# A hybrid GLA, SSD and mixture-of-experts block on one core: attention state per 128 tokens, and expert operands 128 columns wide

## The chip, the core and the metric

The kernel runs on one core of a Trainium2 chip. The metric is device microseconds (us) of one launch; the kernel before takes 2227.91 us (median of three runs, 2227.89 to 2229.29). A core has a matrix engine (TensorE; PE in the profile, its weight loads PEld), three engines for elementwise work (VectorE or DVE, ScalarE or ACT, GpSimd or POOL), a queue engine that issues most transfers (SyncE or SP), and 16 DMA engines between HBM and the on-chip memory. The engines run at the same time, each through its own instructions in program order, and wait for one another by semaphores only.

## What is computed

The reference, cut to what the change touches:

```python
def gla_scan(q, k, v, log_a):                 # one direction, per head; 64 tokens per chunk
    def step(state, inp):
        b = jnp.cumsum(gc, axis=1)            # cumulated log gates inside the chunk
        b_mid = b[:, c // 2][:, None]
        s = where(mask, (qc * exp(b - b_mid)) @ (kc * exp(b_mid - b)).T, 0)
        o = s @ vc + (qc * exp(b)) @ state
        kd = kc * exp(b[:, -1:] - b)
        state = state * exp(b[:, -1]) + kd.T @ vc
...
def moe(xn, w_router, b_router, w1, b1, w2, b2):   # top 4 of 32 experts per token
    def expert_block(xblk, e):
        hdn = xblk @ w1[e] + b1[e]            # 1024 -> 2048
        gate = minimum(hdn[..., :1024], 7.0)
        lin = clip(hdn[..., 1024:], -7.0, 7.0)
        return gate * sigmoid(1.702 * gate) * (lin + 1.0) @ w2[e] + b2[e]   # 1024 -> 1024
```

There are 512 tokens, 4 GLA heads (key width 128, value width 256, both directions), an SSD mixer, and 32 experts. A state that is kept once per 128 tokens gives the same output as one per 64, if the products between the two halves of the 128 are formed as well.

## The kernel before

All data are float32. Large products are made from splits: a matrix is copied to a rounded high half (ACT) and the rest is kept as a low half (DVE subtracts), and three matmuls of 512 columns (high by high, high by low, low by high) stand for one. Products inside the attention are plain float32, and each of them is two matmul records in the trace.

**The mixer stage.** The input projection is cut into 112 *units* of 1024 x 128 weights. Each is loaded by SP (three slots), split by ACT (`split_high`) and DVE (`split_low`), and used by PE in a *piece* of 24 matmuls of 512 columns. SP loads unit n once the low half of unit n - 3 is made. ACT takes each piece out of PSUM (`piece_take`), and a piece waits until the piece two before it was taken. Groups of four units (quads) are needed together.

**The GLA heads** run between pieces, in an order written out by hand (`HEAD_PIECES` for PE and ACT, `HEAD_SPLITS` for DVE). In a head, DVE forms differences of the cumulated gates, ACT takes eight exponentials of 128 x 512, DVE multiplies them with q or k. PE makes scores (L451), transposes the decayed keys (L442), multiplies the masked scores with v (L465), and then walks through eight chunks of 64 tokens, forward and backward together: a state matmul (L479), DVE's update of the state (L582, L585), and the state's share of the output in the next step (L476). The two buffers of exponentials are single, so a head's exponentials wait for the last output matmul of the head before.

**The expert stage** is a loop over 32 experts (a *pass*). The tokens of an expert are gathered by POOL (at most 96 per round, `CAP`), transposed by PE and split into `rows_high` and `rows_low`; these are the stationary operands, with 96 columns each for 8 chunks. The weights stream in as tiles of 128 x 2048 (1 MB) through a ring of eight slots: 8 tiles for the product up, 4 for the product down of the expert before. ACT makes `w_high`, DVE `w_low`, each with three slots, so ACT splits a tile once PE is done with the tile three before. PE runs 12 matmuls of 512 columns per tile. SP loads a tile when DVE has split the tile eight before. Between the tiles DVE clamps gate and linear part (L2020, L2021), makes `rows_low` of the next expert (L1991), the product of gate and linear part (L2032) and `act_low` (L2051). The order on DVE around them is

```python
            gate_dve(v, it)          # both clamps
            rows_dve(v, it + 1)
            if not is_first(it):
                for j in range(UP + 2, TILES):   # the third and the fourth tile of the product down
                    low_dve(v, it, odd, j)
            glu_dve(v, it)
```

After the loop, the last expert's product down is made from four more tiles. Its splits on DVE stand behind `places_dve`, which waits until the previous expert's rows were scattered, and on ACT behind `down_act`, the row scaling of the previous expert.

Of the kernel before, what the change touches and what calls it, by code (L numbers as in the profile page):

```python
# [14 lines left out]
P = 128  # L15
# [30 lines left out]
CAP = 96  # L46
ROUNDS = -(-SEQ // CAP)
# [49 lines left out]
def build(nc, x, norm_mix_g, w_in, fw2_f, fb_f, fw2_b, fb_b, gla_norm_g, conv_w, conv_b, dt_bias_f,  # L97
          dt_bias_b, a_log_f, a_log_b, ssd_d, ssd_norm_g, w_up_gla, w_up_ssd, w_out, norm_ffn_g,
          w_router, b_router, w1, b1, w2, b2, norm_final_g, out):
    with ExitStack() as ctx:  # L100
# [160 lines left out]
        def piece_take(act, n):  # L261
# [4 lines left out]
            if kind in ("q", "k"):  # L266
                if i == 1 and kind == "q":
                    act.wait_ge(scan_ok, 4 + 2 * HEADS)
                if i >= 2:
                    act.wait_ge(g_qk, 8 * (i - 1))  # L270
# [80 lines left out]
        def dts(i):  # L351
# [23 lines left out]
        g_e = [[take(SEQ) for _ in range(4)] for _ in range(2)]  # L375
        at_gd = used[0]
        g_d = [[take(SEQ) for _ in range(2)] for _ in range(2)]
        kd_n = take(2 * SEQ).rearrange("p (d t n) -> p d t n", d=2, t=NT)
        s_m = take(SEQ)
        s_w = take(SEQ // 2)  # L380
        o_junk = take(DV)
        g_st = [take(DV) for _ in range(2)]
        dec = take(2 * NCH).rearrange("p (d c) -> p d c", d=2)
# [18 lines left out]
        LAST, MID = (CH - 1, 0), (CH // 2, CH // 2 - 1)  # L402
# [3 lines left out]
        HEAD_PIECES = ({"start": (8, 9), "score": (), "kd": (), 1: (), 4: (10,), "end": (11,)},  # L406
                       {"start": (12, 13), "score": (14,), "kd": (15,), 1: (16,), 4: (17,), "end": (18, 19)},
                       {"start": (20, 21), "score": (), "kd": (), 1: (), 4: (22,), "end": (23,)},
                       {"start": (24, 25), "score": (26,), "kd": (27,), 1: (28,), 4: (29,), "end": (30, 31, 32, 33)})
# [4 lines left out]
        def o_at(c):  # L414

            t, half = divmod(c, KG)
            return slice(half * CH, (half + 1) * CH), 4 + t // 2, slice((t % 2) * DV, (t % 2 + 1) * DV)
# [12 lines left out]
        def gla_pe(pe, h):  # L430
# [4 lines left out]
            def transposes(d):  # L435
                pe.wait_ge(g_qk, h * 8 + 4 * d + 4)
# [4 lines left out]
                for t in range(NT):  # L441
                    last = nc.tensor.transpose(ps[:, 3, t * P:(t + 1) * P], g_e[d][3][:, t * P:(t + 1) * P], ident[:])  # L442
                last.then_inc(kd_ps, 1)
            transposes(0)
            pe.wait_ge(g_qk, h * 8 + 8)
            for d in range(2):
                for c in range(NCH):
                    rows = o_at(c)[0]
                    to = d * 4 * CH + (c // KG) * CH
                    i = slice(c * CH, (c + 1) * CH)  # L450
                    last = nc.tensor.matmul(ps[rows, 2, to:to + CH], g_e[d][1][:, i], g_e[d][0][:, i], start=True, stop=True)  # L451
# [6 lines left out]
            pe.wait_ge(s_sel, h * 2 + 2)  # L458
# [1830 lines left out]
```

## Time and profile before

| | before |
|---|---|
| runs, median (range) | 2227.91 us (2227.89 to 2229.29) |
| profiled execution: its time, its span | 2231.43 us, 2229.7 us |
| PE, PEld busy | 2046.1 us (92%), 1490.9 us (67%) |
| DVE, ACT, POOL busy | 1603.5 us (72%), 1219.5 us (55%), 263.1 us (12%) |
| moved by DMA | 541.09 MB, mean 243 GB/s |

The span is one execution from first to last instruction; the execution's own time is 1.7 us longer. The heads of the GLA lie at about 84 to 352 us of the span, the expert stage at about 985 to 2200 us. A timeline row gives start, length, engine, line and operation, `out<-in` by the program's names (`temps` is the scratch area in which nearly all of the mixer stage lives, `ps` is PSUM), the shapes, and in brackets the idle time before it with what ended it. A record of a matmul is longer than the distance to the next one, since matmuls overlap: the pace of PE is read from starts.

### The profile page before, as it was taken

The page shows a single profiled execution, that of the slowest core. Times are in us where ns is not written, and L with a number is a line of the kernel's source. Part 1 is how long each engine was busy: PE and PEld are TensorE (multiplying, and loading weights), DVE is VectorE, ACT ScalarE, POOL GpSimd, SP SyncE. Part 2 cuts the span into 40 slices and gives each one's busy share as a digit, 9 for nine tenths or more (in the row PEclk, how much of TensorE's full clock was granted, in tenths as well). Part 3 has the DMA queues.
Part 4 walks back from the last instruction along what each step waited for, and adds up shares of the span by engine and source line. Part 5 has one row for each costly group of instructions (what it writes and reads, how often), then busy time and mean ns, then how long its engine had stood idle before and what let it go on. Part 6 is the DMA issues. An engine that isn't in the chain of part 4 may idle for free. (4 is left out here: it accounts for less than half of the span.)

```text
span 2229.7 us, 26227 instructions
## 1 busy us (share of the span) xinstructions
PE 2046.1 (92%) x9338; PEld 1490.9 (67%) x9338; DVE 1603.5 (72%) x1527; ACT 1219.5 (55%) x1049; POOL 263.1 (12%) x172
## 2 busy tenths in 40 slices
PE   6999897999979999959999999999999999999992
PEld 4766565777766888836666666666666666666661
DVE  5552536787776225257999989898989898989883
ACT  5442423354353323216777777776777777777763
POOL 0000003524513000001101011101100101000000
PEclk9999898999989999959999999999999999999996
DMA  5221314444423943428999999999999999999982
GB/s 134 60 76 38 95 38 152 142 135 139 133 74 109 330 148 114 180 101 309 347 360 362 364 359 366 352 367 356 359 358 363 361 352 359 361 361 360 358 290 83
DMA packets 212051, 541.09 MB, mean 243 GB/s; under 512 B 16439, under 2 KB 131545, under 8 KB 175065
## 3 DMA queue, kind: packets, MB, share of 16 engines
q1 hardware_dynamic: 204600, 518.54, 64.4%
q0 software_dynamic: 7392, 21.77, 4.2%
q8 instruction: 37, 0.61, 0.1%
q14 instruction: 22, 0.17, 0.0%
HBM read 512.87 MB, written 31.59 MB: 244 GB/s over the span
## 5 line engine op out<-in xcount | busy, mean ns | idle before, releaser
L1917 DVE TENSOR_TENSOR w_low<-ring_b,w_high 128x2048 fp32r<-128x2048 f32 x192 | 436.7, 2289 | 56.2 <-ACT w_high L1911 54.7
L1917 DVE TENSOR_TENSOR w_low<-ring_a,w_high 128x2048 fp32r<-128x2048 f32 x192 | 436.3, 2288 | 56.6 <-ACT w_high L1911 55.0
L1911 ACT ACTIVATE w_high<-ring_b 128x2048 fp32r<-128x2048 f32 x192 | 368.1, 1918 | 171.6 <-PE ps L2008 113.3
L1911 ACT ACTIVATE w_high<-ring_a 128x2048 fp32r<-128x2048 f32 x192 | 367.8, 1918 | 165.6 <-PE ps L2008 115.6
L2008 PE MATMUL ps<-w_high,rows_high 128*96 128x512 f32 x1024 | 406.0, 396 | 2.0 <-DVE w_low L1917 2.0
L2008 PE MATMUL ps<-w_high,rows_low 128*96 128x512 f32 x1024 | 403.7, 394 | 0.0
L2008 PE MATMUL ps<-w_low,rows_high 128*96 128x512 f32 x1024 | 402.6, 393 | 0.0
L2066 PE MATMUL ps<-w_high,act_high 128*96 128x512 f32 x512 | 206.0, 402 | 32.3 <-DVE w_low L1917 32.3
L2008 PEld LDWEIGHTS ps<-w_high,rows_high 128*96 128x96 f32 x1024 | 165.8, 162 | 72.7 <-DVE w_low L1917 3.9
L2008 PEld LDWEIGHTS ps<-w_high,rows_low 128*96 128x96 f32 x1024 | 165.7, 162 | 71.9
L2008 PEld LDWEIGHTS ps<-w_low,rows_high 128*96 128x96 f32 x1024 | 166.2, 162 | 69.6
L235 DVE TENSOR_TENSOR unit_low<-unit_raw,unit_high 128x1024 fp32r<-128x1024 f32 x108 | 141.0, 1317 | 98.0 <-ACT unit_high L230 97.8
L240 PE MATMUL ps<-xn_high,unit_high 128*128 128x512 f32 x448 | 187.7, 419 | 22.2 <-ACT temps L289 10.5
L2066 PE MATMUL ps<-w_high,act_low 128*96 128x512 f32 x512 | 201.9, 394 | 0.0
L2066 PE MATMUL ps<-w_low,act_high 128*96 128x512 f32 x512 | 201.3, 393 | 0.0
L230 ACT ACTIVATE unit_high<-unit_raw 128x1024 fp32r<-128x1024 f32 x108 | 111.8, 1053 | 138.4 <-PE ps L242 86.9
L242 PE MATMUL ps<-xn_high,unit_low 128*128 128x512 f32 x448 | 178.2, 398 | 0.0
L241 PE MATMUL ps<-xn_low,unit_high 128*128 128x512 f32 x448 | 177.9, 397 | 0.0
L1966 POOL DMA_INDIRECT residual_rows<-late_b x32 | 46.0, 1439 | 769.5 <-ACT late_b L2076 746.2
L2066 PEld LDWEIGHTS ps<-w_high,act_high 128*96 128x96 f32 x512 | 82.9, 162 | 78.0 <-DVE w_low L1917 46.8
L240 PEld LDWEIGHTS ps<-xn_high,unit_high 128*128 128x128 f32 x448 | 86.4, 193 | 48.8 <-issue 27.5
L1127 POOL TENSOR_TENSOR temps<-temps,dt_all 128x1024 f32<-128x1024 f32 x32 | 71.5, 2262 | 386.4 <-DMA temps<-cum_rows 370.7
(324 smaller groups left out, 2946.1 us busy)
## 6 DMA issues: line engine op xcount, KB each, us to landing
ring_a<-in_w SPq DMA_DIRECT2D x192, 1024.0 KB, 6.9
ring_b<-in_w SPq DMA_DIRECT2D x192, 1024.0 KB, 7.0
unit_raw<-in_w_in SPq DMA_DIRECT2D x80, 512.0 KB, 4.1
temps<-cum_rows SPq DMA_DIRECT2D x16, 1024.0 KB, 7.1
unit_raw<-in_w_up_ssd SPq DMA_DIRECT2D x16, 512.0 KB, 4.5
ssd_out_T<-y_high SPq DMA_DIRECT2D x4, 1024.0 KB, 6.3
ssd_out_T<-y_low SPq DMA_DIRECT2D x4, 1024.0 KB, 6.6
ssd_high<-ssd_out_T SPq DMA_DIRECT2D x4, 1024.0 KB, 11.0
```

What stands on the lines that cost most here:

```text
L230: nc.scalar.activation(dst, raw(n), ACT.Copy).then_inc(u_hi, 1)
L235: nc.vector.tensor_tensor(l[:, slot_cols(n)], raw(n), h[:, slot_cols(n)].bitcast(F32), ALU.subtract).then_inc(u_lo, 1)
L240: nc.tensor.matmul(dst, sh, mh, start=first, stop=False)
L241: nc.tensor.matmul(dst, sh, ml, start=False, stop=False)
L242: return nc.tensor.matmul(dst, sl, mh, start=False, stop=last)
L1127: nc.gpsimd.tensor_tensor(b, b, per_head_i(CUM, t, g, d), ALU.subtract).then_inc(seg, 1)
L1911: nc.scalar.activation(w_hi[:, split_at(it, j)], slot(at, 1)[:, 0, :], ACT.Copy).then_inc(w_hi_ok, 1)
L1917: nc.vector.tensor_tensor(w_lo[:, split_at(it, j)], slot(at, 1)[:, 0, :], w_hi[:, split_at(it, j)].bitcast(F32), ALU.subtract).then_inc(w_ ...
L1966: pool.indirect_dma_start(out=h_d, out_offset=bass.IndirectOffsetOnAxis(ap=to_i[0:CAP, :], axis=0), in_=ye[0:CAP, :], in_offset=None, boun ...
L2008: last = nc.tensor.matmul(ps[0:CAP, n, :], a[:, k, :], w[:, cols], start=False, stop=k == UP - 1 and i == 2)
L2066: last = nc.tensor.matmul(ps[0:CAP, 4 + n, :], a[:, k, :], w[:, cols], start=k == 0 and i == 0, stop=k == NK - 1 and i == 2)
```

## The change

It has four parts. (1) In the GLA, `NT` = 4 tiles of 128 tokens take the place of 8 chunks of 64 in the walk: 3 state updates per direction where there were 7. The scores inside a half are as before; those between the halves of a tile come from a fifth exponential (`OFF`) and eight small matmuls more per head; DVE puts both into one 128 x 128 block per tile. The exponentials are written over their own inputs. (2) The stationary operands of the expert stage (`rows_*`, `act_*`, `pick`) become 128 columns wide; 96 are used, the others are zeroed once before the loop. (3) On DVE the low half of the third tile of the product down moves between the two clamps. (4) After the loop, the splits of the last expert's first three tiles move ahead of the row scaling on ACT, and ahead of `places_dve` on DVE.

```diff
+WIDE = 128
...
     def gla_pe(pe, h):
...
             transposes(0)
-            pe.wait_ge(g_qk, h * 8 + 8)
+            pe.wait_ge(g_qk, h * 12 + 12)
+            if h:
+                pe.wait_ge(st_ok, h * 6)
             for d in range(2):
                 for c in range(NCH):
...
+                    nc.tensor.matmul(ps[half_rows(c % KG), 2, to:to + CH], g_e[d][KS][:, i], g_e[d][QS][:, i], start=True, stop=True)
+                for t in range(NT):
+                    off = by_half(g_e[d][OFF])[:, t]
+                    last = nc.tensor.matmul(off_at(d)[:, t, :], off[:, d, :], off[:, 1 - d, :], start=True, stop=True)
...
-            for c in range(NCH):
-                rows, b, cols = o_at(c)
-                nc.tensor.matmul(ps[rows, b, cols], s_w[rows, (c // KG) * CH:(c // KG + 1) * CH], v_w[h // 2][rows, c // KG, vs],
-                                 start=(c // KG) % 2 == 0, stop=False, skip_group_check=True)
+            for t in range(NT):
+                nc.tensor.matmul(o_at(t), s_w[:, t, :], v_w[h // 2][:, t, vs], start=t % 2 == 0, stop=False, skip_group_check=True)
...
-            for s in range(NCH):
+            for s in range(NT):
...
-                        pe.wait_ge(st_ok, h * 14 + 2 * (s - 1) + d + 1)
-                        last = nc.tensor.matmul(ps[rows, b, cols], g_e[d][2][:, c * CH:(c + 1) * CH], g_st[d],
+                        pe.wait_ge(st_ok, h * 6 + 2 * (s - 1) + d + 1)
+                        last = nc.tensor.matmul(o_at(t), g_e[d][QI][:, tokens(t)], g_st[d],
...
         def gla_exps(act, h, d):
...
+            nc.scalar.activation(g_e[d][QI], cumg[:, at_b:at_b + SEQ], ACT.Exp, scale=1.0 / TAU).then_inc(g_exp, 1)
+            act.wait_ge(g_diff, h * 8 + 4 * d + 4)
+            nc.scalar.activation(g_e[d][KD], g_e[d][KD], ACT.Exp, scale=1.0 / TAU).then_inc(g_exp, 1)
+            nc.scalar.activation(g_e[d][KS], g_e[d][QS], ACT.Exp, scale=-1.0 / TAU).then_inc(g_exp, 1)
+            act.wait_ge(g_exp, h * 10 + 5 * d + 3)
+            nc.scalar.activation(g_e[d][QS], g_e[d][QS], ACT.Exp, scale=1.0 / TAU).then_inc(g_exp, 1)
+            nc.scalar.activation(g_e[d][OFF], g_e[d][OFF], ACT.Exp, scale=1.0 / TAU).then_inc(g_exp, 1)
...
     def gla_dve(v, h):
...
+                nc.vector.tensor_tensor(by_tile(g_e[d][KD]), last, by_tile(b), ALU.subtract).then_inc(g_diff, 1)
...
+                nc.vector.tensor_tensor(by_chunk(g_e[d][QS]), by_chunk(b), mid, ALU.subtract).then_inc(g_diff, 1)
...
+                nc.vector.tensor_tensor(off[:, :, d, :], edge, b4[:, :, d, :], ALU.subtract).then_inc(g_diff, 1)
+                nc.vector.tensor_tensor(off[:, :, 1 - d, :], b4[:, :, 1 - d, :], edge, ALU.subtract).then_inc(g_diff, 1)
...
             nc.vector.copy_predicated(s_m, gmask.bitcast(U32), ps[:, 2, :]).then_inc(s_sel, 1)
-            v.wait_ge(s_sel, h * 2 + 1)
-            nc.vector.tensor_tensor(s_w, s_m[:, 0:SEQ // 2], s_m[:, SEQ // 2:SEQ], ALU.add).then_inc(s_sel, 1)
+            for u in range(KG):
+                rows = half_rows(u)
+                nc.vector.tensor_copy(s_w[rows, :, half_rows(1 - u)], off_at(u)).then_inc(s_sel, 1)
+            v.wait_ge(s_sel, h * 5 + 1)
+            for u in range(KG):
+                rows = half_rows(u)
+                both = s_m[rows, :].rearrange("p (d t i) -> p d t i", d=2, t=NT)
+                nc.vector.tensor_tensor(s_w[rows, :, rows], both[:, 0], both[:, 1], ALU.add).then_inc(s_sel, 1)
...
-                if s == 2:
+                if s == 1:
                     for n in splits["loop"]:
                         split_low(v, n)
...
-        x_hi, x_lo = (small_r(n, NK * CAP) for n in ("rows_high", "rows_low"))
-        a_hi, a_lo = (small_r(n, NK * CAP) for n in ("act_high", "act_low"))
+        x_hi, x_lo = (small_r(n, NK * WIDE) for n in ("rows_high", "rows_low"))
+        a_hi, a_lo = (small_r(n, NK * WIDE) for n in ("act_high", "act_low"))
...
+                for a in (x_hi, x_lo, a_hi, a_lo):
+                    spare = a[:, :].rearrange("p (c w) -> p c w", c=NK)[:, :, CAP:WIDE]
+                    nc.vector.memset(spare.bitcast(F32), 0.0).then_inc(b1_lo, 1)
+                nc.vector.memset(pick[:, CAP:WIDE].bitcast(F32), 0.0).then_inc(b1_lo, 1)
...
-                        last = nc.tensor.matmul(ps[0:CAP, n, :], a[:, k, :], w[:, cols], start=False, stop=k == UP - 1 and i == 2)
+                        last = nc.tensor.matmul(ps[:, n, :], a[:, k, :], w[:, cols], start=False, stop=k == UP - 1 and i == 2)
...
             gate_dve(v, it)
+            if not is_first(it):
+                low_dve(v, it, odd, UP + 2)
+            linear_dve(v, it)
             rows_dve(v, it + 1)
             if not is_first(it):
-                for j in range(UP + 2, TILES):
-                    low_dve(v, it, odd, j)
+                low_dve(v, it, odd, UP + 3)
             glu_dve(v, it)
...
                 acts_act(act, end - 1)
+                for j in range(DOWN - 1):
+                    high_act(act, end, 0, j)
                 down_act(act, end - 1, TILES, before * 16)
-                for j in range(DOWN):
-                    high_act(act, end, 0, j)
+                high_act(act, end, 0, DOWN - 1)
...
                 acts_dve(v, end - 1)
+                for j in range(DOWN - 1):
+                    low_dve(v, end, 0, j)
                 places_dve(v, end - 1)
-                for j in range(DOWN):
-                    low_dve(v, end, 0, j)
+                low_dve(v, end, 0, DOWN - 1)
```

`HEAD_PIECES` keeps its pieces; those that stood behind step 1 and step 4 of eight now stand behind step 0 and step 1 of four. Three places of the programs, as the engines will run them. First PE's walk through the state of head 0, from the product of scores and v (L465) to the piece that stood behind step 4; before:

```order
L465 MATMUL ps<-temps_64 64x256 x8
L479 MATMUL ps<-temps_64 128x256 x2
L476 MATMUL ps<-temps_64 64x256
L479 MATMUL ps<-temps_64 128x256
L476 MATMUL ps<-temps_64 64x256
L479 MATMUL ps<-temps_64 128x256
```

and now, complete up to the piece (the product of scores and v is now L479, the state L491, the state's share of the output L488):

```order
L479 MATMUL ps<-temps_64 128x256 x4
L491 MATMUL ps<-temps_64 128x256 x2
L488 MATMUL ps<-temps_64 128x256
L491 MATMUL ps<-temps_64 128x256
L488 MATMUL ps<-temps_64 128x256
L491 MATMUL ps<-temps_64 128x256
L241 MATMUL ps<-xn_high_59,unit_high_62 128x512
```

Before, the pair L476 and L479 comes eight times ahead of that piece and four times behind it, then L476 twice; now it comes twice ahead and twice behind, then L488 twice. Second, DVE in a pass around the clamps; before:

```order
L1917 TENSOR_TENSOR w_low_7309<-ring_a_5680,w_high_7308 128x2048
L2020 TENSOR_SCALAR late_c_5679<-ps 96x1024
L2021 TENSOR_SCALAR late_c_5679<-ps 96x1024
L1991 TENSOR_TENSOR rows_low_7311<-ps,rows_high_7310 128x768
L1916 REGISTER_ALU
L1917 TENSOR_TENSOR w_low_7309<-ring_a_5680,w_high_7308 128x2048
L1916 REGISTER_ALU
L1917 TENSOR_TENSOR w_low_7309<-ring_a_5680,w_high_7308 128x2048
L2031 ISA
L2032 SCALAR_TENSOR_TENSOR late_c_5679<-late_c_5679 96x1024
```

and now (L1951 is the low half of a tile, L2057 and L2064 the clamps):

```order
L1951 TENSOR_TENSOR w_low_7196<-ring_a_5567,w_high_7195 128x2048
L2057 TENSOR_SCALAR late_c_5566<-ps 96x1024
L1950 REGISTER_ALU
L1951 TENSOR_TENSOR w_low_7196<-ring_a_5567,w_high_7195 128x2048
L2064 TENSOR_SCALAR late_c_5566<-ps 96x1024
L2028 TENSOR_TENSOR rows_low_7198<-ps,rows_high_7197 128x8x96
L1950 REGISTER_ALU
L1951 TENSOR_TENSOR w_low_7196<-ring_a_5567,w_high_7195 128x2048
L2074 ISA
L2075 SCALAR_TENSOR_TENSOR late_c_5566<-late_c_5566 96x1024
```

The first of the two low halves stands one clamp and `rows_low` earlier; the second keeps its place. Third, ACT after the loop; before:

```order
L2047 ACTIVATE act_high<-ps 128x768
L2073 REGISTER_ALU
L2074 REGISTER_ALU
L2076 ACTIVATE late_b<-ps,late_b 96x1024
L1908 REGISTER_ALU
L1910 ISA
L1911 ACTIVATE w_high<-ring_b 128x2048
```

and now (L2119 is the row scaling, L1945 the high half of a tile):

```order
L2090 ACTIVATE act_high<-ps 128x8x96
L1942 REGISTER_ALU
L1944 ISA
L1945 ACTIVATE w_high<-ring_b 128x2048
L1944 REGISTER_ALU
L1945 ACTIVATE w_high<-ring_b 128x2048
L1944 REGISTER_ALU
L1945 ACTIVATE w_high<-ring_b 128x2048
L2116 REGISTER_ALU
L2117 REGISTER_ALU
L2119 ACTIVATE late_b<-ps,late_b 96x1024
```

Three high halves have passed the row scaling; on DVE three low halves have passed `places_dve` in the same way.

## Rows read from the trace of the kernel before

**Rows 1.** Windows: length, busy PE, PEld, DVE, ACT, POOL (count), clock, DMA share, GB/s
```profile
229.00:241.00 12.00, 7.73 (x58) 4.94 (x58) 8.95 (x13) 5.48 (x8) 0.00 (x0) 0.50 0.50 132
...
728.00:784.00 56.00, 56.00 (x248) 46.34 (x247) 13.64 (x12) 19.38 (x19) 0.00 (x0) 1.00 0.93 323
945.00:950.00 5.00, 1.30 (x7) 1.16 (x6) 2.75 (x20) 2.68 (x3) 1.91 (x5) 0.50 1.01 428
1008.00:2173.00 1165.00, 1138.57 (x5289) 801.48 (x5289) 1045.53 (x758) 826.35 (x502) 108.23 (x62) 1.00 0.97 354
```

**Rows 2.** Waits, 1200 to 2150 us: in total, times, longest
```profile
ACT w_high L1911 <- PE ps L2008: 182.8, 206, 2.0
...
PE ps L2066 <- DVE w_low L1917: 17.6, 26, 0.7
```

**Rows 3.** Timeline of PE: one pass of the expert loop and its period
```profile
1313.32 0.82 PE L1982 MATMUL ps<-ident,late_c 96*128 96x96 f32 x8
...
1320.37 0.48 PE L2066 MATMUL ps<-w_high,act_high 128*96 128x512 f32 x1 [0.68 <-DVE w_low L1917]
...
1327.58 0.39 PE L2008 MATMUL ps<-w_high,rows_high 128*96 128x512 f32 x1
...
1335.65 0.40 PE L2008 MATMUL ps<-w_high,rows_low 128*96 128x512 f32 x1
...
1350.10 0.82 PE L1982 MATMUL ps<-ident,late_c 96*128 96x96 f32 x8
```

**Rows 4.** Groups by form: weight loads of 96 (1200 to 2150) and 128 columns
```profile
L2008 PEld LDWEIGHTS ps<-w_high,rows_high 128*96 128x96 f32 x822 | 132.6, 161 | 56.4 <-DVE w_low L1917 1.3
...
L240 PEld LDWEIGHTS ps<-xn_high,unit_high 128*128 128x128 f32 x145 | 27.9, 192 | 15.9 <-issue 7.7 <-DVE unit_low L235 2.7
```

**Rows 5.** Timeline of DVE: the same pass around the clamps
```profile
1314.91 1.21 DVE L2020 TENSOR_SCALAR late_c<-ps 96x1024 f32<-96x1024 f32 x1
1316.04 1.21 DVE L2021 TENSOR_SCALAR late_c<-ps 96x1024 f32<-96x1024 f32 x1
...
1318.03 4.48 DVE L1917 TENSOR_TENSOR w_low<-ring_b,w_high 128x2048 fp32r<-128x2048 f32 x2
```

**Rows 6.** Timeline of PE: the walk through the state of head 0
```profile
113.37 1.94 PE L465 MATMUL ps<-temps 64*64 64x256 f32 x16
...
116.45 0.65 PE L476 MATMUL ps<-temps 128*64 128x256 f32 x2 [0.51 <-DVE temps L582]
...
126.07 0.50 PE L240 MATMUL ps<-xn_high,unit_high 128*128 128x512 f32 x1
...
131.74 0.65 PE L476 MATMUL ps<-temps 128*64 128x256 f32 x2
...
137.76 0.50 PE L240 MATMUL ps<-xn_high,unit_high 128*128 128x512 f32 x1
```

**Rows 7.** Timeline, start of head 1: differences, exponentials, scores
```profile
148.97 2.49 DVE L554 TENSOR_TENSOR temps<-temps 128x512 f32<-128x512 f32 x4
...
150.29 4.29 ACT L500 ACTIVATE temps<-temps 128x512 f32<-128x512 f32 x8 [0.66 <-DVE temps L554]
...
157.76 1.15 PE L451 MATMUL ps<-temps 128*64 128x64 f32 x32 [1.96 <-DVE temps L564]
```

**Rows 8.** Timeline of PE: the piece that waits for head 0's exponentials
```profile
96.64 0.76 PE L240 MATMUL ps<-xn_high,unit_high 128*128 128x512 f32 x1 [5.26 <-ACT temps L277]
```

**Rows 9.** Timeline of DVE: clearing 64 x 2048 ahead of the expert stage
```profile
980.18 1.76 DVE L1813 MEMSET bias_split<- 64x2048 f32 x1 [0.48 <-issue]
```

**Rows 10.** Timeline of ACT, DVE and PE after the loop
```profile
2174.59 1.10 ACT L2076 ACTIVATE late_b<-ps,late_b 96x1024 f32<-96x1024 f32 x1
2175.59 5.50 ACT L1911 ACTIVATE w_high<-ring_b 128x2048 fp32r<-128x2048 f32 x3
...
2182.73 6.70 DVE L1917 TENSOR_TENSOR w_low<-ring_b,w_high 128x2048 fp32r<-128x2048 f32 x3
...
2185.07 0.74 PE L2066 MATMUL ps<-w_high,act_high 128*96 128x512 f32 x1 [11.31 <-DVE w_low L1917]
```

More of the change, by code:

```diff
@@ L374, in build @@
         at_ge = used[0]
-        g_e = [[take(SEQ) for _ in range(4)] for _ in range(2)]
-        at_gd = used[0]
-        g_d = [[take(SEQ) for _ in range(2)] for _ in range(2)]
+        QS, KS, QI, KD, OFF = range(5)
+        g_e = [[take(SEQ) for _ in range(5)] for _ in range(2)]
+        at_gd = at_ge + 8 * SEQ
         kd_n = take(2 * SEQ).rearrange("p (d t n) -> p d t n", d=2, t=NT)
         s_m = take(SEQ)
-        s_w = take(SEQ // 2)
+        s_w = take(SEQ).rearrange("p (t i) -> p t i", t=NT)
         o_junk = take(DV)
         g_st = [take(DV) for _ in range(2)]
-        dec = take(2 * NCH).rearrange("p (d c) -> p d c", d=2)
+        dec = take(2 * NT).rearrange("p (d t) -> p d t", d=2)
         at_o = used[0]
@@ L400, in build, with by_tile, by_half, half_rows @@
         cum_T = T[:, at_o + 8 * NT * 64:at_o + 8 * NT * 64 + SEQ]
[L402 to L409, printed above, removed]
+        LAST, MID, EDGE = (P - 1, 0), (CH // 2, CH // 2 - 1), (CH - 1, CH)
+        HEAD_PIECES = ({"start": (8, 9), "score": (), "kd": (), 0: (), 1: (10,), "end": (11,)},
+                       {"start": (12, 13), "score": (14,), "kd": (15,), 0: (16,), 1: (17,), "end": (18, 19)},
+                       {"start": (20, 21), "score": (), "kd": (), 0: (), 1: (22,), "end": (23,)},
+                       {"start": (24, 25), "score": (26,), "kd": (27,), 0: (28,), 1: (29,), "end": (30, 31, 32, 33)})
         def by_chunk(ap):
             return ap.rearrange("p (c i) -> p c i", i=CH)
[L414 to L417 removed]
+        def by_tile(ap):
+            return ap.rearrange("p (t i) -> p t i", t=NT)
+        def by_half(ap):
+            return ap.rearrange("p (t u i) -> p t u i", t=NT, u=KG)
+        def half_rows(u):
+            return slice(u * CH, (u + 1) * CH)
+        def o_at(t):
+            return ps[:, 4 + t // 2, (t % 2) * DV:(t % 2 + 1) * DV]
+        def off_at(u):
+            return ps[half_rows(u), 6, DV:2 * DV].rearrange("p (t i) -> p t i", t=NT)
         def takes(act, ns):
@@ L518, in gla_act @@
                 dt_exps(act)
+            takes(act, at_step[0])
             takes(act, at_step[1])
-            takes(act, at_step[4])
             act.wait_ge(o_ps, h + 1)
@@ L2000, in up_pe @@
             for n in range(4):
-                nc.tensor.matmul(ps[0:CAP, n, :], pick[:, :], b1_s[:, n * 512:(n + 1) * 512], start=True, stop=False)
+                nc.tensor.matmul(ps[:, n, :], pick[:, :], b1_s[:, n * 512:(n + 1) * 512], start=True, stop=False)
             for k in range(UP):
@@ L2065, in down_pe @@
                         for i, (a, w) in enumerate(((aT_hi, w_hi), (aT_hi, w_lo), (aT_lo, w_hi))):
-                            last = nc.tensor.matmul(ps[0:CAP, 4 + n, :], a[:, k, :], w[:, cols], start=k == 0 and i == 0, stop=k == NK - 1 and i == 2)
+                            last = nc.tensor.matmul(ps[:, 4 + n, :], a[:, k, :], w[:, cols], start=k == 0 and i == 0, stop=k == NK - 1 and i == 2)
                 last.then_inc(w_used, 1)
```

102 lines of the change are left out of this document (53 added, 49 removed).

## The prediction, made before the changed kernel ran

> **What bounds the kernel now.** I read the windows by stage first, then the waits of the expert loop, then its timeline on PE and DVE, then the timeline of the heads. The windows [rows 1] give the loop over the experts 1165 us of a span of 2229.7, with PE busy 1139, DVE 1046, and a DMA share of 0.97. Three resources look full; the waits separate them. ACT waits for PE to free a slot of `w_high` (206 times, 0.9 us each), and in this stretch it never waits for a landing tile; PE waits for DVE once per pass (26 times in 950 us, 0.68 us each) [rows 2]. So PE sets the pace, except at one place per pass, the third tile of the product down, where DVE does. One pass lasts 1350.10 - 1313.32 = 36.78 us [rows 3]. PE's own part: from 1327.58 to 1335.65 lie 35 starts, 0.2306 us apart [rows 3], with 148 such matmuls in a pass (34.1 us), and 2.7 us of small ones and the wait.
>
> In the heads PE is busy too. The walk of head 0 runs from 113.37 to 126.07 and from 131.74 to 137.76: 18.7 us without the piece between [rows 6]. DVE's update hides beside PE there: the only wait is 0.51 us at the first step.
>
> **Part 1, the state per 128 tokens.** The last stretch of the walk [rows 6] holds ten float32 products in 6.02 us, 0.60 each. Half of them have 64 stationary columns, half 128. Now there are 4 products with v, 6 for the state and 6 for its share of the output, all 128 by 128: 16. The trace has no such product of 256 columns; 0.60 is the nearest, and I take 0.62, with 0.50 and 0.70 as ends. 16 x 0.62 + 0.5 us of wait = 10.4 us against 18.7: 8.3 us less per head, 33.2 in four.
>
> Against it stands what is added at the edges of a head, where the walk before has to end first.
> - Differences: DVE made four in 2.49 us [rows 7]; now four full and four half ones, about 3.85 us with 0.36 for a half (my estimate, from 0.62 for a full one; at most 0.62). ACT makes ten exponentials instead of eight, 0.54 each [rows 7], and waits for itself once per direction, since one overwrites its input; behind that wait stand its other exponentials, for which DVE waits. One exponential per direction needs no difference and goes first. In head 0, PE waits 5.26 us for the piece taken behind the exponentials [rows 8]: + 1.5 us.
> - Multiplications: eight full and four half ones. The scores of head 1 waited 1.96 us for DVE [rows 7]. DVE is now 1.35 later after the differences and has 1.5 more to multiply, less 1.15 of waits that shrink, since the exponentials are ready when it comes: + 1.7 us in head 1, and in head 2, which starts alike.
> - Scores: eight small products more, about 0.8 us, and two copies and one addition more on DVE before the block is whole, about 1.05. Pieces cover the block in heads 1 and 3, and DVE's splits cover the products in head 1. Head 0 pays 1.85, head 3 0.8, head 2 1.4 more, since PE is granted the lower of its two clocks (1.2 of 2.4 GHz) there, 0.50 from 229 to 241 us [rows 1], and another 1.0 in the product with v for the same reason.
> - Head 3: the low half of unit 29 comes behind the second update instead of the third, and the piece that needs it now comes right behind: PE waits about 1.75 us, less 0.65 for the wait at the first step, which a piece now covers. What is queued behind is that piece and the third step, for which DVE waits.
>
> Sum: - 33.2 + 1.5 + 1.85 + 1.7 + 1.7 + 2.4 + 0.8 + 1.1 = - 22.2 us. The walk that shrinks also moves two loads: DVE's low halves behind the walk free the slots for the next unit, and they move with it. Ends: with 0.50 per product - 30, with 0.70 - 17; with all edges twice as dear - 11.
>
> **Parts 2 and 3, a pass of the expert loop.** Width first. At 96 stationary columns the starts are 0.2306 us apart; in the window from 728 to 784 PE does nothing but matmuls of 512 columns at 128 columns, 248 in 56 us, 0.2258 apart (0.2267 if one record is missing), and that at a DMA share of 0.93 [rows 1]. So neither transfers nor anything of the splits explains the 96: I take 4.2 ns less per matmul, 0 and 4.8 as ends. The weight load gets longer, 161 to 192 ns [rows 4], and still fits beside 227 ns.
>
> The Trainium skill ("TensorE: Matmul & The Clock Gate", "Back-to-back issue gap") lets the gap depend on the moving columns alone, N / 2.4 + 2.5 ns, 215.8 ns at 512. By it a wider stationary operand brings nothing; this trace shows 230.6 and 225.8, neither of them 215.8.
>
> Then the order on DVE. Before: the low half of tile 10 ends at 1314.9, clamps 1.13 each, `rows_low` 0.86, low half of tile 11 from 1318.03 to 1320.3 [rows 5]; PE starts on it at 1320.37 where it could have at 1319.5 [rows 3]. Now: clamp to 1316.04, low half to 1318.3, clamp to 1319.4, `rows_low` to 1320.3, low half of tile 12 to 1322.5. Tile 11 is then in time. Tile 12 is the one that comes late: PE could start it at 1322.1 and starts at 1322.55, where before it started at 1323.23: 0.7 us earlier. What width gives between is swallowed by that wait. Behind it 100 matmuls are left in the pass, 100 x 4.2 ns = 0.42 us. The rest of DVE's work (three low halves, `act_low`) keeps its times, and each is done 1.0 us or more before PE asks. So 1.12 us per pass, 36.78 to 35.66; 31 passes: - 34.7 us. The pass of the first expert has no product down: - 0.4. Ends: width worth nothing, 0.70 per pass, - 21.7; the third tile's wait gone and no new one, 1.45 per pass, - 45.
>
> Clearing the spare columns: 256 elements per partition, four times, and 32 once, at the pace of 1.76 us for 2048 [rows 9]: 1.2 us, and the stage behind starts when DVE ends: + 1.2.
>
> **Part 4, after the loop.** Before, DVE waited for the scatter, began the low halves at 2182.73, and PE began at 2185.07 after 11.31 us without work [rows 10]. Now ACT makes three high halves from 2174.6 to 2180.1, then scales (1.1 us) to 2181.2; the first low half is done at 2178.8. What is late next is the scaling, which frees the PSUM that PE writes: PE starts at 2181.2. Its four tiles take as long as before. The fourth low half now waits for the scatter that starts 5.5 us later, lands at about 2188.1 and is split by 2190.6, just before PE needs it at 2190.9. - 3.9 us.
>
> **Sum:** - 22.2 - 0.4 - 34.7 + 1.2 - 3.9 = - 60.0 us. The profiled execution took 2231.4, so 2171.4; the median of the runs lies 3.5 lower, so 2168.
>
> **Rivals.**
> - *Width brings nothing.* For it: the difference is 2%, and the two stages differ in more than width. Against it: the window at the same DMA share. It takes 0.42 x 31 + 0.4 = 13.4 us back: 2181.
> - *The edges of the heads eat more.* DVE and ACT end each chain that starts a head; if they are twice as dear, 11 us: 2179. For it: only few rows price the half operations; PE's clock falls after such waits.
> - *DMA becomes the bound of the loop.* A pass moves 354 GB/s x 36.78 us = 13.0 MB. At a share of 1.00 that is 354 / 0.97 = 365 GB/s, 35.67 us, which is just what I forecast; a little less capacity in the steady state, and the gain stops there. Half of the loop's gain lost: 2186. Against it: 428 GB/s in a window of 5 us with a filled queue [rows 1], and ACT never waits for a tile. The Trainium skill ("DMA: Bandwidth & Descriptors", "Specifications") gives a limit of about 358 GB/s per core from HBM; by it a pass would take at least 36.4 us and the kernel about 2191. The 428 GB/s speak against it.
> - *Slower: the longer weight load shows.* It is hidden only as long as it fits beside the matmul before. If its 31 ns were added to each of 4736 matmuls of the expert stage, 147 us, and the 14 us that width brings were gone, the kernel would take 2168 + 14 + 147 = 2329; it turns slower from 46 / 4736, about 10 ns per matmul, on. Against it: the window of 248 matmuls with loads of 192 ns.
> - *Nothing happens in the loop*: no wait goes, since `rows_low` moved back delays the transposes. The transposes of the gated product come 3.4 us after it; no sign of this. 2203.
>
> **How the numbers follow.** Forecast 2168, 55%, with its own range 2158 to 2178. Width nothing 13%; edges 12%; DMA 10%; nothing in the loop 3%; slower by the weight load, or by a wait that I did not find, 4%; more than forecast (2150 to 2158) 3%. The range that leaves out 2 in 10 at most is 2156 to 2190. About 0.2% is what a measurement of this kernel can tell from no change. All cases but the slower one end below 2223, with 0.01 left for a loss of almost everything: faster 0.95, same 0.01, slower 0.04.
>
> **What would show it.** The walk: 16 products per head at about 0.62 and 10.4 us; if they take 0.7 or more, that step is wrong. The starts of the expert stage's matmuls 0.2265 apart. The wait of PE for DVE once per pass, now ahead of the fourth tile down, under 0.5 us; period 35.7. PE's start after the loop 8 us after the last transposes instead of 12. A wait of ACT's high halves for DMA, or starts that stay at 0.2306, would make the prediction wrong.

## The result, and the profile after

| | kernel before | changed kernel |
|---|---|---|
| median of the runs, us | 2227.9 (2225.5 to 2229.3) | 2167.7 (2166.3 to 2170.2) |
| profiled execution, us | 2231.4, span 2229.7 | 2166.3, span 2164.6 |
| first product behind head 3, TensorE | 363.58 | 327.69 |
| period of a pass without disturbance; mean over the loop | 36.78; 36.82 | 35.98; 36.05 |
| last transposes of the loop to TensorE's next start | 12.13 | 8.38 |

The ratio is 0.9734, 95% interval 0.9719 to 0.975: 60 us faster, 2168 was forecast. The two profiled executions lie 65.1 us apart, because that of before was 3.5 us over its median and that of after 1.4 under it. This is how the 65.1 us divide:

| stretch | forecast | traces |
|---|---|---|
| four heads (363.58 to 327.69) | - 22.2 | - 35.9 |
| rest of the mixer, router | 0 | - 2.0 |
| clearing the spare columns | + 1.2 | + 1.2 |
| loop, from VectorE's slot selection (985.50; 948.86) to the last transposes (2172.94; 2111.57) | - 35.1 | - 24.7 |
| behind the loop | - 3.9 | - 3.7 |

So the total was met by two misses of opposite sign, 13.7 us too little in the heads and 10.4 too much in the loop: that it came within 1 us is luck. The row of the heads is itself uncertain by a few us. The same code of the heads reaches the product behind head 3 between 322.95 and 329.65 us in the eight traces that have it; what goes with that is told at the head of the experiments.

The timeline of TensorE in head 0 of the changed kernel (start, duration, line, tile, shapes, count, wait before it; two records make one float32 product):

```profile
98.02 0.77 PE L241 MATMUL ps<-xn_high,unit_high 128*128 128x512 f32 x1 [6.73 <-ACT temps L278]
...
116.05 3.64 PE L479 MATMUL ps<-temps 128*128 128x256 f32 x8 [1.90 <-DVE temps L602]
119.53 1.03 PE L491 MATMUL ps<-temps 128*128 128x256 f32 x4
...
122.28 0.58 PE L241 MATMUL ps<-xn_high,unit_high 128*128 128x512 f32 x1
...
127.96 0.59 PE L488 MATMUL ps<-temps 128*128 128x256 f32 x2
128.39 0.59 PE L491 MATMUL ps<-temps 128*128 128x256 f32 x2
128.82 0.59 PE L488 MATMUL ps<-temps 128*128 128x256 f32 x2
129.25 0.59 PE L491 MATMUL ps<-temps 128*128 128x256 f32 x2
129.68 1.44 PE L488 MATMUL ps<-temps 128*128 128x256 f32 x4
130.77 0.58 PE L241 MATMUL ps<-xn_high,unit_high 128*128 128x512 f32 x1
```

Read the starts, not the durations, since neighbours overlap: 127.96, 128.39, 128.82, 129.25, 129.68 are 0.43 us apart, where [rows 6] had 0.60. The first four products (116.05 to 119.53) take 0.87 each, behind the wait, where TensorE is granted the lower of its two clocks, 1.2 of 2.4 GHz (the 0.50 in this window, columns as in [rows 1]; from 127 to 131 us it is 1.00):

```profile
116.00:119.00 3.00, 2.95 (x7) 2.42 (x8) 2.36 (x2) 2.40 (x5) 0.00 (x0) 0.50 0.13 27
```

In low_first, an experiment below with the same heads, these four take 0.46 each at a granted clock of 1.00:

```profile
115.31 1.99 PE L479 MATMUL ps<-temps 128*128 128x256 f32 x8 [1.89 <-DVE temps L602]
117.14 1.03 PE L491 MATMUL ps<-temps 128*128 128x256 f32 x4
```

The walk of head 0 lasts 6.23 + 2.81 = 9.0 us instead of 18.7. Over the four heads (without waits of pieces) it falls from 77.5 to 33.0 us.

The edges came as forecast in kind: the piece behind head 0's exponentials waits 6.73 instead of 5.26 us [rows 8], and the scores of heads 1 and 2 wait for DVE's multiplications, head 1's 3.18 instead of 1.96 [rows 7]:

```profile
152.24 0.69 PE L463 MATMUL ps<-temps 128*64 128x64 f32 x16 [3.18 <-DVE temps L588]
...
215.83 1.12 PE L463 MATMUL ps<-temps 128*64 128x64 f32 x16 [6.11 <-DVE temps L588]
```

One pass of the loop on TensorE, and what VectorE does there; these answer to [rows 3] and [rows 5]:

```profile
1306.64 0.83 PE L2019 MATMUL ps<-ident,late_c 96*128 96x96 f32 x8
...
1315.31 0.39 PE L2109 MATMUL ps<-w_high,act_low 128*128 128x512 f32 x1
1315.93 0.50 PE L2109 MATMUL ps<-w_high,act_high 128*128 128x512 f32 x1 [0.24 <-DVE w_low L1951]
1316.27 0.39 PE L2109 MATMUL ps<-w_low,act_high 128*128 128x512 f32 x1
...
1321.11 0.39 PE L2045 MATMUL ps<-w_high,rows_high 128*128 128x512 f32 x1
...
1328.37 0.39 PE L2045 MATMUL ps<-w_high,rows_low 128*128 128x512 f32 x1
...
1342.62 0.83 PE L2019 MATMUL ps<-ident,late_c 96*128 96x96 f32 x8
```

```profile
1311.60 1.21 DVE L2064 TENSOR_SCALAR late_c<-ps 96x1024 f32<-96x1024 f32 x1
1312.74 0.94 DVE L2028 TENSOR_TENSOR rows_low<-ps,rows_high 128x768 fp32r<-128x768 f32 x1
1313.60 2.28 DVE L1951 TENSOR_TENSOR w_low<-ring_a,w_high 128x2048 fp32r<-128x2048 f32 x1
```

TensorE's wait for VectorE stands ahead of the fourth tile down: 0.24 us are listed, but against a spacing of 0.23 the start at 1315.93 is 0.39 late, and the matmul behind it comes 0.34 later instead of 0.23. From 1321.11 to 1328.37 lie 32 intervals of 0.2269. The waits of 1150 to 2100 us, columns as in [rows 2]:

```profile
PE ps L2109 <- DVE w_low L1951: 6.3, 26, 0.2
```

```profile
ACT w_high L1945 <- PE ps L2045: 181.9, 213, 1.3
```

Behind the loop TensorE starts when ScalarE's row scaling has freed the PSUM, as forecast (compare [rows 10]); the first three low halves begin at 2115.15, the scatter's wait of 5.48 us is now beside TensorE's work:

```profile
2111.57 0.82 PE L2082 MATMUL ps<-ident,late_c 96*128 96x96 f32 x8
2119.95 0.79 PE L2109 MATMUL ps<-w_high,act_high 128*128 128x512 f32 x1 [7.56 <-ACT late_b L2119]
```

### The profile page after: what moved, and what is told of

Same layout as the page of the kernel before. It is cut to its first block and busy times, and to the rows that moved or that the text cites. A ratio compares the mean times of both kernels' runs of the same rounds, so it can differ in the third digit from the quotient of the medians.

```text
span 2164.6 us, 26048 instructions
## 1 busy us (share of the span) xinstructions
PE 1992.0 (92%) x9242; PEld 1610.8 (74%) x9242; DVE 1607.6 (74%) x1544; ACT 1225.3 (57%) x1057; POOL 245.8 (11%) x172
## 5 line engine op out<-in xcount | busy, mean ns | idle before, releaser
L1951 DVE TENSOR_TENSOR w_low<-ring_a,w_high 128x2048 fp32r<-128x2048 f32 x192 | 435.4, 2286 | 42.2 <-ACT w_high L1945 41.8
L1951 DVE TENSOR_TENSOR w_low<-ring_b,w_high 128x2048 fp32r<-128x2048 f32 x192 | 435.7, 2286 | 40.8 <-ACT w_high L1945 40.5
L1945 ACT ACTIVATE w_high<-ring_b 128x2048 fp32r<-128x2048 f32 x192 | 368.2, 1919 | 155.6 <-PE ps L2045 109.3
L1945 ACT ACTIVATE w_high<-ring_a 128x2048 fp32r<-128x2048 f32 x192 | 367.9, 1918 | 151.9 <-PE ps L2045 109.6
L2045 PE MATMUL ps<-w_high,rows_high 128*128 128x512 f32 x1024 | 403.7, 394 | 1.3 <-DVE w_low L1951 1.3
L2045 PE MATMUL ps<-w_high,rows_low 128*128 128x512 f32 x1024 | 400.3, 391 | 0.0
L2045 PE MATMUL ps<-w_low,rows_high 128*128 128x512 f32 x1024 | 399.5, 390 | 0.0
L2045 PEld LDWEIGHTS ps<-w_high,rows_high 128*128 128x128 f32 x1024 | 193.0, 188 | 44.1 <-DVE w_low L1951 4.6
L2045 PEld LDWEIGHTS ps<-w_high,rows_low 128*128 128x128 f32 x1024 | 192.6, 188 | 41.1
L2045 PEld LDWEIGHTS ps<-w_low,rows_high 128*128 128x128 f32 x1024 | 193.1, 189 | 39.6
L2109 PE MATMUL ps<-w_high,act_high 128*128 128x512 f32 x512 | 207.0, 404 | 15.2 <-DVE w_low L1951 7.6
L241 PE MATMUL ps<-xn_high,unit_high 128*128 128x512 f32 x448 | 187.2, 418 | 25.8 <-ACT temps L290 10.5
L2109 PE MATMUL ps<-w_high,act_low 128*128 128x512 f32 x512 | 200.5, 392 | 0.0
L2109 PE MATMUL ps<-w_low,act_high 128*128 128x512 f32 x512 | 200.1, 391 | 0.0
L2109 PEld LDWEIGHTS ps<-w_high,act_high 128*128 128x128 f32 x512 | 96.5, 188 | 47.0 <-DVE w_low L1951 28.9
```

The lines of the kernel that those rows point to most:

```text
L241: nc.tensor.matmul(dst, sh, mh, start=first, stop=False)
L1945: nc.scalar.activation(w_hi[:, split_at(it, j)], slot(at, 1)[:, 0, :], ACT.Copy).then_inc(w_hi_ok, 1)
L1951: nc.vector.tensor_tensor(w_lo[:, split_at(it, j)], slot(at, 1)[:, 0, :], w_hi[:, split_at(it, j)].bitcast(F32), ALU.subtract).then_inc(w_ ...
L2045: last = nc.tensor.matmul(ps[:, n, :], a[:, k, :], w[:, cols], start=False, stop=k == UP - 1 and i == 2)
L2109: last = nc.tensor.matmul(ps[:, 4 + n, :], a[:, k, :], w[:, cols], start=k == 0 and i == 0, stop=k == NK - 1 and i == 2)
```

## The experiments

Besides the medians of whole executions, the traces give each kernel's periods: the "mean" is over the 29 or 30 passes of the loop, "undisturbed" the value that most or the quickest of them show. Executions of one code differ by some us ahead of the loop: in the eight traces whose code there is the same but for the clearing, TensorE's first slot product starts between 944.7 and 953.8 us. The granted clock goes with it. Ahead of that product TensorE is at the lower clock for 113 to 126 us in the five traces that reach it by 948.8, and for 133 to 137 us in the three that reach it later, the changed kernel's among them (summed from the granted clock that each trace lists). So a few us are read from the loop, not from the medians.

| kernel | columns | undisturbed | mean | median, us |
|---|---|---|---|---|
| before | 96 | 36.78 | 36.82 | 2227.9 |
| pass_back | 96 | 36.76 | 36.79 | 2189.3 |
| order_back | 128 | 36.50 | 36.56 | 2181.8 |
| width_96 | 96 | 36.21 | 36.23 | 2168.6 |
| changed | 128 | 35.98 | 36.05 | 2167.7 |
| low_first_96 | 96 | 35.84 | 35.89 | 2159.3 |
| low_first_112 | 112 | 35.74 | 35.94 | 2161.5 (one run) |
| low_first | 128 | 35.44 | 35.70 | 2156.7 |
| heads_early | 128 | 35.44 | 35.77 | 2138.4 |
| places_late | 128 | 35.44 | 35.44 | 2131.2 |

**Width, order and end, undone one at a time.**

```
width_96:    WIDE = 96, outputs ps[0:WIDE, ...], nothing cleared
order_back:  gate_dve; linear_dve; rows_dve; low_dve(UP + 2); low_dve(UP + 3)
pass_back:   both
ends_back:   down_act, places_dve ahead of all four splits of the last expert
```

> Only the width goes back: rows, acts and pick are 96 columns wide again, everything else stays as changed. Theory A (a matmul of 512 columns starts 3.5 to 4 ns later after the one before it when its stationary operand has 96 instead of 128 columns): 36 of the 148 matmuls of a pass stand ahead of the fourth tile of the product down, whose wait swallows what they lose; the other 112 cost 0.40 us per pass, so a period of 36.4 instead of 35.98 and about 2180 us, 12 us slower than the changed kernel; starts 0.2305 apart again. Theory B (the width brings nothing, the order on VectorE did it all): 2168, within 2 us. Theory C (the longer weight load of 128 columns costs something that the changed kernel pays): faster than 2166.

> Only the order on VectorE goes back: both clamps and rows_low ahead of the low half of the third tile of the product down, 128 columns kept. Theory A (VectorE sets when the third tile can start, 7.05 us behind the transposes as before the change, and with it the fourth at 9.87 instead of 9.29): 0.5 to 0.6 us per pass, 31 passes, about 2184 us; the wait of TensorE for w_low stands ahead of the third tile again and is longer than before the change, since TensorE comes there sooner. Theory B (DMA at a share of 1.00 holds the changed pass at 35.98, so the order's gain was partly lost to it): giving the order back costs less than 0.3 us per pass, 2177 or less.

> Width and order both go back, the attention state per 128 tokens and the end behind the loop stay as changed. Theory A (the two parts are worth 0.80 us per pass together, as the two traces have it, 36.78 against 35.98): 24.8 us slower than the changed kernel, about 2192.5. Theory B (the pass would have come to 35.66 as forecast but for something outside these two parts): 2202.

> Only the end behind the loop goes back: row scaling and places ahead of all four splits of the last expert. Theory A (TensorE has nothing to do until the first low half, and the end of the kernel hangs on TensorE's last product): 3.7 us slower, about 2171.5, with TensorE starting 12.1 us behind the last transposes. Theory B (the scatter of the last expert's rows ends the chain anyway): no difference, 2168 within 1.

Measured, as ratios to before: width_96 0.9744 (0.9731 to 0.9758), order_back 0.9795 (0.9782 to 0.9809), pass_back 0.9823 (0.981 to 0.9837), ends_back 0.9751 (0.9738 to 0.9765).

The order is worth 36.76 - 36.21 = 0.55 us per pass at 96 columns and 36.50 - 35.98 = 0.52 at 128: theory A holds there (2181.8 against 2184 expected). The width is worth 0.26 without the new order and 0.23 with it: theory A's 0.40 fell, and so did "nothing". The median alone would not have told: 2168.6 is only 0.9 us over the changed kernel, as "nothing" had it. From VectorE's slot selection to the last transposes the traces have 1168.8 us against 1162.7, 6.0 more; against that, the loop begins 4.3 us earlier in this trace, 1.2 of it since nothing is cleared and the rest within what executions differ by there. The trace of width_96 shows why it is less:

```profile
1304.21 0.82 PE L2015 MATMUL ps<-ident,late_c 96*128 96x96 f32 x8
...
1312.95 0.40 PE L2105 MATMUL ps<-w_high,act_low 128*96 128x512 f32 x1
1313.46 0.47 PE L2105 MATMUL ps<-w_high,act_high 128*96 128x512 f32 x1
1313.77 0.39 PE L2105 MATMUL ps<-w_low,act_high 128*96 128x512 f32 x1
...
1340.42 0.82 PE L2015 MATMUL ps<-ident,late_c 96*128 96x96 f32 x8
```

The fourth tile starts 9.25 us behind the transposes, with 128 columns 9.29: VectorE sets it in both. No wait is listed here, yet the start is 0.28 late (0.51 behind its neighbour instead of 0.23); a wait that is not listed is still one. What is left behind it is 26.96 us against 26.69, 0.27 less for 112 matmuls, as the mean spacing is 0.2310 at 96 and 0.2278 at 128, 3.2 ns and not 4.2, and four bias products and the restart give some back.

Pass_back lands at 2189.3 with theory A's 2192.5 nearer than B's 2202. In ends_back TensorE starts 12.18 us behind the last transposes, 3.80 more than in the changed kernel (8.38), which is theory A; from the last transposes to the end of the span it takes 56.9 us against 53.0. Its median is 5.5 us up, more than these 3.8, and its traced execution has the latest start of the loop of the eight.

**The state of the attention, undone; and what a float32 product costs.**

```
state_back:   lines of the attention as before the change, all else as changed
probe_mixed:  head 1: kd_n[0:64, d, t, :] x v[0:64]           (state: 64 rows)
              head 3: g_e[d][QI][:, 64 columns] -> ps[0:64]    (share: 64 columns)
              head 2: both
probe_alike:  head 1: state and share with 64 rows
              head 3: state and share with 64 columns
```

Both probes leave out parts of the sums; the number and order of the products stay.

> The kernel before with the other parts alone: 128 columns and VectorE's order in the pass, and the splits ahead of the row scaling, while the attention state goes back to 64 tokens per chunk. Theory A (the heads gave 36 us, as the two traces have it): 35 to 37 us slower than the changed kernel, about 2204. Theory B (the heads gave the 22 us that were forecast, and the rest of the 36 is how far two executions differ ahead of the loop): 2190.

> The changed kernel with some float32 products of the walk cut in size (part of the sums is left out, the count of instructions stays): in head 1 the products for the state take 64 of 128 rows, in head 3 the shares of the output write 64 of 128 rows (64 stationary columns), in head 2 both, which is the alternation of the kernel before. To be read: how far the starts lie apart where TensorE is at its full clock. Theory A (a product over half the array is dearer by itself): the cut ones take 0.57 to 0.63 us, the full ones between them 0.43, so a pair 1.0 to 1.06 in heads 1 and 3 and 1.20 in head 2. Theory B (going from one shape of stationary operand to another costs, whichever it is): both kinds take 0.6, a pair 1.2 in heads 1, 2 and 3. Theory C (what was dear before was something else, as the walk's order): 0.43 everywhere.

> The changed kernel with the products of the walk cut alike (part of the sums is left out): in head 1 the products for the state and the shares of the output both take 64 of 128 rows with 128 columns, in head 3 both have 128 rows with 64 columns, so that no shape follows another within a run of products. Theory A (half the array is dearer by itself): 0.63 in head 1 and 0.57 in head 3. Theory B (the change of shape costs): 0.43 in both, except for the first one of each run. Theory C: 0.43 everywhere.

state_back took 2205.7 us, ratio 0.9901 (0.9885 to 0.9916), 38 us over the changed kernel: the heads did give the 36 us of the traces, not 22. The probes tell why; TensorE is granted its full clock (1.00) in all four stretches shown. First probe_mixed, head 1 and then head 3, where one of two neighbours is cut; then probe_alike, the same heads, where both are cut alike (L495 is the share of the output, L499 the state; 64*128 is 64 rows and 128 stationary columns):

```profile
175.06 0.70 PE L499 MATMUL ps<-temps 64*128 64x256 f32 x2
175.68 0.70 PE L495 MATMUL ps<-temps 128*128 128x256 f32 x2
176.31 0.70 PE L499 MATMUL ps<-temps 64*128 64x256 f32 x2
...
283.15 0.70 PE L499 MATMUL ps<-temps 128*128 128x256 f32 x2
283.78 0.65 PE L495 MATMUL ps<-temps 128*64 128x256 f32 x2
284.36 0.70 PE L499 MATMUL ps<-temps 128*128 128x256 f32 x2
```

```profile
183.39 0.59 PE L499 MATMUL ps<-temps 64*128 64x256 f32 x2
183.82 0.59 PE L495 MATMUL ps<-temps 64*128 64x256 f32 x2
184.26 0.59 PE L499 MATMUL ps<-temps 64*128 64x256 f32 x2
...
280.35 0.59 PE L499 MATMUL ps<-temps 128*64 128x256 f32 x2
280.78 0.59 PE L495 MATMUL ps<-temps 128*64 128x256 f32 x2
281.21 0.59 PE L499 MATMUL ps<-temps 128*64 128x256 f32 x2
```

In the first a pair takes 1.25 and 1.21 us, and the full product beside a cut one is as dear as its neighbour (0.63). In the second every product takes 0.43, cut or not. So theory B holds: the shape itself costs nothing, going from one shape to another costs 0.14 to 0.20 us, each time. The walk of before changed shape at almost every product behind those with v; that of after never does. The eight products with v of before were cheap: in head 0 their records start in pairs, one for each half of the 128 rows, and all eight take 1.87 us (113.37 to 115.24). The four that replace them take as long at 0.43 each, 1.7 us. The Trainium skill ("TensorEngine Tiling (Array Packing)", "Key Properties") says that changing the tiling mode, and not just the tile, drains TensorE; the runs fit that, and 0.14 to 0.20 us is their price for it.

**What holds the pass now.** The fourth tile's low half ahead of rows_low, then the same with 96 and with 112 columns.

```
 linear_dve(v, it)
+low_dve(v, it, odd, UP + 3)
 rows_dve(v, it + 1)
-low_dve(v, it, odd, UP + 3)
```

> The changed kernel with VectorE's low half of the fourth tile of the product down ahead of rows_low, which TensorE needs only 4.5 us later. Theory A (VectorE alone holds the fourth tile back, by 0.39 us in each pass, and nothing else is full): the wait of TensorE for w_low goes, period 35.98 to about 35.6, 31 passes, 11 us: 2157. Theory B (DMA, at a share of 1.00 of the time, holds the pass): period unchanged at 35.9 to 36.0, ACT's high halves begin to wait for landing tiles, 2167. Theory C (the wait of 0.24 goes, but not the 0.1 us that a first matmul behind a gap costs): 35.75, 2160.

> The kernel with the fourth tile's low half ahead of rows_low, and with 96 columns instead of 128. Theory A (the width is worth 3.3 to 3.8 ns in every matmul of a steady run, and nothing swallows it once no tile is late): the period goes from 35.67 to about 36.05, 0.38 per pass, 31 passes less 1.2 us for the clearing that is not needed: 10.5 us slower than low_first, about 2167. Theory B (the width is worth only the 0.2 us per pass that width_96 showed): 35.87, about 2162. Theory C (VectorE needs 35.6 us per pass anyway or DMA does): no difference.

> The same with 112 columns: to be read is how far the starts of the matmuls lie apart in the steady run behind the third tile. Theory A (a stationary operand that is not full costs a fixed amount): 0.2305 as at 96. Theory B (the cost goes with the missing columns): 0.2286, half way to 0.2267.

low_first: 0.9683 (0.967 to 0.9696), theory A's 2157; undisturbed passes take 35.44. low_first_96: 0.9699 (0.9686 to 0.9712), undisturbed 35.84: with no late tile the width is worth 0.40 us per pass, theory A's 0.38. But the means differ by 0.19 only and the medians by 2.6 us, not 10.5: the faster kernel has something else that holds it, and passes of 35.4 to 36.3. In low_first_112 the mean spacing is 0.2306, against 0.2309 at 96 and 0.2277 at 128: nearer to theory A, a fixed cost of not being full. One such pass of low_first, VectorE and TensorE:

```profile
1182.69 0.15 DVE L1984 CAST late_b<-late_b 96x1 int32 x1 [0.74 <-DMA residual_rows<-late_b]
...
1184.32 4.49 DVE L1951 TENSOR_TENSOR w_low<-ring_a,w_high 128x2048 fp32r<-128x2048 f32 x2
```

```profile
1186.66 0.50 PE L2045 MATMUL ps<-w_high,rows_high 128*128 128x512 f32 x1 [0.42 <-DVE w_low L1951]
```

VectorE's places (two copies of one column for the next scatter) wait until the scatter before has landed; behind them stand the slot selection and the low halves of the last tiles up, and TensorE waits for one of these. It is listed 11 times in 25 passes of low_first and twice in 25 of the changed kernel, whose passes are longer. The pass grows by what VectorE waits: 36.16 us with the 0.74 shown above (TensorE's transposes at 1156.09 and 1192.24), 36.25 with the longest, 0.79, and 35.44 in the passes without any.

**A faster version.**

```
heads_early:  low_first, and piece_take(6) ahead of head 0's exponentials; high half of unit 23
              behind the output's in head 1; low half of unit 22 behind head 2's
              multiplications; 29 ahead of head 3's updates; both halves of
              units 34 to 37 (and load 37) inside head 3
places_late:  + places_dve behind the low half of the last tile up
```

> low_first with five moves of waits in the heads, no work added: the gate piece 6 is taken ahead of the exponentials of head 0; the high half of unit 23 behind the output's high half in head 1; the low half of unit 22 behind all multiplications of head 2; the low half of unit 29 ahead of the first update in head 3; the halves of units 34 to 37 (the SSD stage's first quad) as soon as they can be made instead of behind head 3. Theory A (each of these waits of TensorE ends with the instruction that I move): head 0's wait of 6.7 us shrinks to 1.4 and with it the stretch at half clock, - 7; head 2's wait of 6.1 us by 3; head 3's 1.7 gone; the 10.5 us behind head 3 shrink to about 2.5, - 8 or a little more with the clock: together 19 to 21 us, about 2137. Theory B (the stage behind is held by VectorE's and ScalarE's own chain from the end of head 3, not by TensorE): the gain of 8 behind head 3 is lost there, about 2145. Theory C (loads of weights hold the heads): less than 5 us in all.

> heads_early with one more move in the pass: VectorE's two small copies for the next scatter (places) go behind the low half of the last tile of the product up, since in low_first VectorE waited there for the scatter before to land, 11 times in 25 passes, up to 0.74 us. In low_first the passes take between 35.44 and 36.25 us, 35.70 on average. Theory A (what lies over 35.44 comes from that wait, which makes the low halves of the last tiles up late): the passes come to 35.44 to 35.5 and the kernel 7 to 9 us down, about 2130. Theory B (what lies over 35.44 comes from DMA, at a share of 0.99, in other ways too, as tiles that land late): the average stays near 35.7 and the time at 2138.

heads_early: 2138.4 us, 0.9604 (0.959 to 0.9617), 18.3 below low_first: theory A, a little short. Head 0's wait is 1.30 instead of 6.73, and the 10.5 us behind head 3 are 4.42; head 3's 1.71 is gone. Head 2 gave under 1 us of the 3 expected: its scores wait 2.38 instead of 6.11, but now the transposes behind them wait 4.29 for ScalarE, where the product with v waited 1.43. Theory B fell: from the product behind head 3 to VectorE's slot selection it takes 622.4 us against 621.1 in low_first, so the stages behind start earlier and end earlier. places_late: 2131.2 us, 0.9567 (0.9553 to 0.9581), theory A: every pass takes 35.44, and TensorE waits for nothing. Its window in the loop (columns as in [rows 1]) and two starts of one pass and the next:

```profile
1008.00:1958.00 950.00, 950.00 (x4502) 788.23 (x4501) 887.93 (x645) 707.71 (x430) 92.59 (x54) 1.00 1.00 373
```

```profile
1184.00 0.82 PE L2024 MATMUL ps<-ident,late_c 96*128 96x96 f32 x8
...
1219.44 0.82 PE L2024 MATMUL ps<-ident,late_c 96*128 96x96 f32 x8
```

## Why the prediction was right in the sum and wrong in two terms

- *"The trace has no such product of 256 columns; 0.60 is the nearest, and I take 0.62, with 0.50 and 0.70 as ends."* The mis-sized term. It measured 0.43, below my lower end. The row was right, but it priced products that alternate in shape (six of 64 columns and four of 64 rows, not half and half), which is a property of the neighbours and not of the product. The sixteen products were counted rightly. At 0.43, and 0.87 for four products each in heads 0 and 2, the walk falls by 11.1 us per head on average, not 8.3.
- *The edges*, + 11.0: walk and heads together leave 44.5 - 35.9 = 8.6, give or take the few us by which executions differ there. Head 0's exponentials + 1.5 (measured 1.47) and the wait for head 3's low half 1.75 (1.71 at 284.12) were right; the scores of head 1, + 1.7, measured 1.2.
- *"So 1.12 us per pass"*: measured 0.80 undisturbed. The order, 0.70 in my sum, gave 0.52 to 0.55: the fourth tile does start 0.62 earlier behind the transposes (9.29 against 9.91), but I let the restart be free, and behind it the second matmul comes 0.11 late. The width, 0.42, gave 0.23: the spacing gains 3.2 ns on average (3.7 in steady runs, 0.2306 to 0.2269) and not the 4.2 that I took from another stage. I had also counted 100 matmuls behind the wait where there are 112, with the fourth tile's own. With nothing swallowed it gives 0.40, as low_first shows.
- *The late tile*: that the fourth would take the third's place, under 0.5 us, was right (0.39). The wait at VectorE's places, which cost low_first 0.26 us per pass on average (35.70 against 35.44), was not in my list. The same wait makes most of the 0.07 by which the mean of the changed kernel is longer than its undisturbed pass: its three longest passes behind the first, 36.25, 36.30 and 36.50 us, are those in which VectorE waits longest there, 0.29, 0.33 and 0.53 us.
- *Clearing* + 1.2 and *the end* - 3.9 were right (1.2; 3.7, and 3.80 by ends_back).
- The rivals: "width brings nothing" and "DMA becomes the bound" did not come. I had put the ceiling at 365 GB/s, 35.67 us; places_late runs at 35.44 with 373 GB/s and no engine waiting for a landing tile. A share of 1.00 did not mean that DMA was the bound. The limit of about 358 GB/s that the prediction took from the Trainium skill ("DMA: Bandwidth & Descriptors", "Specifications") does not hold for this one core. Nor did the longer weight load show.

## What to carry to other kernels

Price a product from a row in which its neighbours have its own shape, and count the changes of shape as a term of their own. When a wait is removed, price the restart behind it and look for the next one on the same engine, down to one-column copies that wait for a transfer. A gain in pace is only worth what no fixed wait swallows: measure it again when the waits are gone.

## What the runs showed of the hardware

- Float32 products of 256 columns at full clock: 0.43 us at 128 by 128, at 64 rows and at 64 columns alike; 0.57 to 0.63 where the shape differs from that of the product before.
- Fp32r matmuls of 512 columns, mean of close starts between 1060 and 1900 us: 0.2310 at 96 stationary columns, 0.2306 at 112, 0.2278 at 128. Why a stationary operand that is not full costs 3 ns stays open; no run here takes the weight load (161 ns at 96, 188 at 128) apart from it.
- The second matmul behind a stall or another operation starts 0.31 to 0.34 us after the first instead of 0.23, even where no wait is listed.
- One core alone held 373 GB/s over 950 us, at a DMA share of 1.00, while TensorE waited for nothing.
- The stretch ahead of the loop differs by up to 9.1 us between executions of the same code, and the time at the lower clock differs with it (113 to 137 us). In the heads the walk shows it: the four products with v of head 0 take 0.87 us each in the changed kernel's trace and 0.46 in low_first's. Why one execution is granted the lower clock for longer than another stays open.
